# A depthwise convolution's shifted copies: sixteen on-chip transfers per block, or five by way of DRAM

## The reference

```python
glu = z[..., :o1] + b_glu
u = glu[..., :D_CONV] * jax.nn.sigmoid(glu[..., D_CONV:])
...
uc = jnp.concatenate([u_past, u], axis=1)
y = lax.conv_general_dilated(uc, w_dw[:, None, :], window_strides=(1,), padding='VALID',
                             dimension_numbers=('NWC', 'WIO', 'NWC'),
                             feature_group_count=D_CONV) + b_dw
y = jax.nn.silu(layer_norm(y, ln_g, ln_b))
return y @ w_pw + b_pw, uc[:, -(CONV_WIDTH - 1):]
```

## Time and profile before

| | us |
|---|---|
| median of 3 runs | 2307.46 |
| all runs | 2057.3, 2307.46, 2405.7 |
| the profiled execution's own time | 2060.45 |
| its span (slowest core, core 0) | 2058.9 |
| the other even cores (2, 4, 6) | 2051.0, 2048.2, 2048.6 |
| the odd cores (1, 3, 5, 7) | 1991.4, 1991.4, 1993.9, 1990.5 |
| PE busy on core 0 | 1924.8 (93%) |
| DVE, ACT, POOL busy on core 0 | 799.2, 366.5, 152.1 |

### The profile page before, as it was taken

One profiled execution on the slowest core, in us unless ns is written; L12 is line 12 of the kernel. 1 busy time (PEld: TensorE's weight loads), 2 busy tenths in 40 slices (PEclk: granted clock), 3 DMA queues, 4 the chain that ended last, 5 costly groups with the idle time before them and its releaser, 6 DMA issues.

```text
span 2058.9 us, 33059 instructions; the slowest of 8 cores (1990.5 to 2058.9 us)
## 1 busy us (share of the span) xinstructions
PE 1924.8 (93%) x12474; PEld 1119.9 (54%) x12474; DVE 799.2 (39%) x1349; ACT 366.5 (18%) x679; POOL 152.1 (7%) x176
## 2 busy tenths in 40 slices
PE   4789899987878999999999999999999999999997
PEld 2344454654544566666446565655656556565653
DVE  2546656644424622223243414234142341423126
ACT  2422121321222522222043000000000000000013
POOL 0000100110111010000000000000000000000000
PEclk9999999999989999999999999999999999999999
DMA  7853766996776386467867997877967556544404
GB/s 199 168 90 73 139 136 144 219 195 133 121 122 90 45 134 98 77 119 117 236 82 148 165 184 123 168 128 135 184 112 121 78 78 83 79 72 61 77 5 165
DMA packets 218970, 252.28 MB, mean 123 GB/s; under 512 B 8944, under 2 KB 190896, under 8 KB 214788
## 3 DMA queue, kind: packets, MB, share of 16 engines
q0 software_dynamic: 193216, 137.77, 49.3%
q1 hardware_dynamic: 22973, 66.01, 9.8%
q10 hardware_dynamic: 2616, 46.28, 7.8%
HBM read 365.16 MB, written 58.67 MB: 206 GB/s over the span
## 4 chain that ended last, share of the span: by engine, by line
PE 86%; DMA 5%; DVE 3%; issue 2%; ACT 2%; SPq 1%; ACTq 1%; DVEq 0%; POOL 0%; POOLq 0%
PE ps L202 86%; SPq L223 1%; DMA aW<-w_in 1%; DMA aU<-aubb 1%; DMA aq<-aqlow 1%; DMA ardb<-dnd 1%; DVE auP L202 1%; ACTq L223 0%; DMA atab<-tab 0%; DVE ahb L202 0%; ACT ahb L202 0%; DMA dnd<-aden 0%; DVE axacc L202 0%; ACT L202 0%; ACT ajunk L202 0%
## 5 line engine op out<-in xcount | busy, mean ns | idle before, releaser
L202 PE MATMUL ps<-amixT,aHW 128*128 128x352 bf16 x4224 | 632.0, 313 | 0.0
L202 PEld LDWEIGHTS ps<-amixT,aHW 128*128 128x128 bf16 x4224 | 412.9, 98 | 218.2 <-issue 0.2
L202 PE MATMUL ps<-ahT,aW 128*128 128x352 bf16 x2304 | 372.1, 321 | 1.8 <-DVE aubb L202 1.0
L202 PE MATMUL ps<-aHW,aaq 128*128 128x512 bf16 (+1 forms) x1584 | 318.2, 380 | 1.4 <-DVE aaq L202 0.4
L202 PEld LDWEIGHTS ps<-ahT,aW 128*128 128x128 bf16 x2304 | 228.2, 100 | 128.2 <-issue 3.8
L202 PE MATMUL ps<-aW,ahT 128*128 128x512 bf16 (+1 forms) x1296 | 283.4, 390 | 7.9 <-DMA aW<-w_in 4.8
L202 DVE TENSOR_TENSOR aaq<-ps,asgb 128x352 bf16<-128x352 f32 x132 | 69.3, 525 | 553.8 <-PE ps L202 553.8
L202 DVE TENSOR_TENSOR axacc<-ps,axacc 128x512 f32<-128x512 f32 x320 | 220.2, 691 | 66.1 <-PE ps L202 34.7
L202 PEld LDWEIGHTS ps<-aHW,aaq 128*128 128x128 bf16 (+1 forms) x1584 | 140.8, 98 | 176.4 <-issue 11.4
L202 PEld LDWEIGHTS ps<-aW,ahT 128*128 128x128 bf16 (+1 forms) x1296 | 133.9, 112 | 135.9 <-issue 25.5
L202 ACT ACTIVATE asgb<-ps 128x352 f32<-128x352 f32 x132 | 61.2, 464 | 819.8 <-PE ps L202 819.7
(11 more groups left out here) (156 smaller groups left out, 1088.9 us busy)
## 6 DMA issues: line engine op xcount, KB each, us to landing
aW<-w_in POOLq DMA_DIRECT2D x40, 1024.0 KB, 13.2
aHW<-w_gate POOLq DMA_DIRECT2D x22, 1024.0 KB, 11.0
aHW<-w_up POOLq DMA_DIRECT2D x22, 1024.0 KB, 17.4
aHW<-w_down POOLq DMA_DIRECT2D x22, 1024.0 KB, 13.6
aKr<-ck SPq DMA_DIRECT2D x36, 512.0 KB, 6.3
aVb<-cv POOLq DMA_DIRECT2D x36, 256.0 KB, 5.8
axb<-xown SPq DMA_DIRECT2D x8, 1024.0 KB, 8.7
axacc<-xown SPq DMA_DIRECT2D x8, 1024.0 KB, 14.4
```

The source lines that it names most:

```text
L202: self.q[eng].append(lambda e: getattr(e, meth)(*a, **kw).then_inc(s, 1))
```

## The change

`conv_in` no longer makes 16 copies on chip. One transfer writes the whole of `ubb[i_]` (128 rows of 1056 bf16 values) to a DRAM tensor `ubd[i_]`, and four transfers read it back, one for each shift `i`, each filling 32 partitions of `U4[i_]` for all four channel groups. The four wait for the write through the key `('ub', i_)`. All five are issued on SP's queue, in both roles and all blocks. In role a `conv_hist` is gone as a function; its steps stand in `rows_out`: first the row transpose, then the two history transposes, then ACT's copy of the history, of the rows, and of the new columns into `uc`. In `later` there is one function per block in place of two.

```diff
     def conv_in(n):
         i_ = n % 2
         S.op('dve', lambda e: e.tensor_tensor(out=dgc[i_], in0=mkap(idr, [[0, 32], [1, 32]]), in1=mkap(wtap[:, n, 0:1], [[1, 32], [0, 32]]), op=ALU.mult))
-        for g in range(4):
-            for i in range(4):
-                S.dma('act' if n >= 6 and not H and i % 2 else 'sp', U4[i_][32 * i:32 * i + 32, g, :], ubb[i_][32 * g:32 * g + 32, 8 * i:8 * i + 1032])
+        S.dma('sp', io['ubd'][i_], ubb[i_], writes=[('ub', i_)])
+        for i in range(4):
+            S.dma('sp', U4[i_][32 * i:32 * i + 32, :, :], bass.AP(io['ubd'][i_].tensor, 8 * i, [[1056, 32], [32 * 1056, 4], [1, 1032]]), reads=[('ub', i_)])
...
     def rows_out(n):
         rb_ = rowb[n % 2][0:NR, :]
         S.op('pe', lambda e: e.transpose(out=PS[6][0:NR, 0:128], in_=u2[n % 2][:, TGG[2][1] - NR:TGG[2][1]], identity=identf))
+        if not H:
+            c_ = uc[n % 2]
+            for a in range(2):
+                S.op('pe', lambda e: e.transpose(out=PS[6][:, 128 + 120 * a:248 + 120 * a], in_=straw[0:120, a, 128 * n:128 * n + 128], identity=identf[0:120, 0:120]))
+            S.op('act', lambda e: e.copy(out=c_[:, :, 0:30], in_=PS[6][:, 128:368].rearrange("p (s r) -> p s r", r=30)))
         S.op('act', lambda e: e.copy(out=rb_, in_=PS[6][0:NR, 0:128]))
         if H:
             S.dma('sp', io['convp'][:, 128 * n:128 * n + 128], rb_)
         else:
+            S.op('act', lambda e: e.copy(out=c_[:, :, 30:34], in_=u2[n % 2][:, 320:352].rearrange("p (s j) -> p s j", j=4)))
             S.dma('sp', bass.AP(io['convs'].tensor, 26 * 1024 + 128 * n, [[30 * 1024, 8], [1024, 4], [1, 128]]), rb_)
-
-    def conv_hist(n):
-        c_ = uc[n % 2]
-        for a in range(2):
-            S.op('pe', lambda e: e.transpose(out=PS[6][:, 128 + 120 * a:248 + 120 * a], in_=straw[0:120, a, 128 * n:128 * n + 128], identity=identf[0:120, 0:120]))
-        S.op('act', lambda e: e.copy(out=c_[:, :, 0:30], in_=PS[6][:, 128:368].rearrange("p (s r) -> p s r", r=30)))
-        S.op('act', lambda e: e.copy(out=c_[:, :, 30:34], in_=u2[n % 2][:, 320:352].rearrange("p (s j) -> p s j", j=4)))
...
                     conv_in(n)
-                    if not H:
-                        later.append(lambda: conv_hist(n))
                     later.append(lambda: rows_out(n))
...
+    io['ubd'] = [nc.dram_tensor("ubd%d" % i, [128, 1056], BF16).ap() for i in range(2)]
```

## The result

| | before | after |
|---|---|---|
| median of all runs, us | 2182.38 | 2030.11 |
| runs compared, us | 2054.83, 2057.3 | 2025.27, 2025.30, 2034.91 |
| the profiled execution, us | 2060.45 | 2034.91 |
| ratio, 95% interval | | 0.9863 [0.9818, 0.9908] |

The kernel became 1.4% faster, 28 us, and the interval keeps clear of 1 by twice its own half width. (In some executions one die's cores are held at a lower clock; these carry the median of before up to 2182 and are left out of every ratio, and of the medians given for the experiments.)

What follows compares the result with a forecast made beforehand. Role a's cores set the end, with 44.5 us of PE idle and lower clock from 455 to 680 us to win. Core 0: 5.0 + 4.0 + 7.9 - 0.3 + 8.1 + 4.5 = 29.2 off 2060.45, forecast 2031, range 2022 to 2046.

Steps and rivals of the forecast that it cites:

- the 8.98 at block 3's `aubb`: DVE's 8.98 us wait in block 1 for the copies before writing aubb for block 3; forecast to be gone.
- Everything hides: Rival, chance 0.18: Kr load in time, trip 7.1 us; block 1 gives 9.3, block 7 6.6; 2019.5 us.
- The round trip starves beside the weight loads: Rival, chance 0.12: at block 1 SP's ring moves 46 GB/s, Kr lands 15 us later; 2051 us.
- the bound of resolution: Claim that a measurement can tell about 2%, 41 us, from no change; chances 0.16 faster, 0.80 between, 0.04 slower.
- block 3, transposes: Row transpose no longer waits for ACT's copies into uc: 3.5 us of wait plus 1.5 of clock, 5.0 gained.
- block 4, conv: Convolution's 5.43 us wait for aU goes, plus 2.7 for faster matmuls: 8.1 gained on core 0.
- block 6, ACT's issues: PE's 6.38 us idle behind ACT's copy issues and copy into uc goes, plus 1.5 of clock: 7.9.
- block 7: 8.35 us gained, less a new 5.9 wait for the reads and 2.7 of slower matmuls: -0.3, bounds -5.4 to +6.6.
- block 1: Of 9.3 us on offer, 3.5 kept plus 1.0 of clock, as the stall moves to a late Kr load: 4.5.
- other small waits (the rest of the stage): Five further PE waits for auc, 5.5 us in all, less 1.5 left for a late u2: 4.0 gained.
- 5.1 and some 4: Block 1's write: 5.1 us for itself, some 4 for reads and a Kr load ahead; lands at about 481.
- the 0.3 for SP's wake-up: Allowance of 0.3 us in the DRAM trip, between the write's landing and the reads; quiet trip 11.3 us.

Runs made afterwards that it cites:

- after_again: The changed kernel run once more with no further change, on the same chip as later experiments: 2026.78 us, ratio 0.9871.
- fill_later: The changed kernel with the four reads of blocks 0 to 3 in role a issued one piece of columns later on SP's queue: 2019.55 us, ratio 0.9836.
- rows_only: The kernel before with only the new order of row and history transposes, the sixteen on-chip copies kept: 2041.87 us, ratio 0.9937.
- all_on_sp: The kernel before with all sixteen copies of every block issued on SP's queue, none on ACT's: 2047.65 us, ratio 0.9969.

## Why the prediction was right or wrong

**The time was right, and most of the mechanism, but part of that was luck.** 2031 was forecast; the runs lie at 2025.3 to 2034.9. These signs came: no wait for `auc`, no issues on ACT, the 8.98 at block 3's `aubb` replaced (7.34, and for the write), a wait before conv(7) of 6.69 where 5.9 stood, a product late through a Kr load near 490 (494.93). Others did not, or came from the list of what would be wrong: SP's waits for the write are 6.2 us on average and up to 10.7, not 3 to 5; the write took over 8 us up to the issue of its reads at three of core 0's eight blocks (8.1, 11.3 and 8.6 at blocks 0, 1 and 3); and conv(5) waited on core 6. The luck is that two terms missed in opposite directions, as the table below shows, and that the slowest run's 2034.91 was set by core 6, for which nothing had been forecast.

"Everything hides" fell at both of its places, block 1 and block 7. "The round trip starves beside the weight loads" fell by the view of the DMA queues on core 0 (packets, MB, share of 16 engines). Block 1's weight load goes out at 471.68 before and at 463.08 after, so what answers the earlier trace rows is the stretch from 462.4 to 483.4:

```profile
q1 hardware_dynamic: 953, 1.96, 35.2%
```

1.96 MB in 21 us is 93 GB/s, where before it was 100, beside the same 2.2 MB on the queue of the weight loads: SP's queue neither starved nor gained. The forecast's 100 GB/s about held, and the rival's 46 did not come.

**The step that failed is the bound of resolution**, "about 2% is what a measurement of this kernel can tell from no change", and with it the 0.80 on a time that can't be told from no change. What the runs showed in its place is a gain of 1.4% with an interval that keeps clear of 1. The intervals here are ±0.45% for the change and ±0.14 to 0.29% for the experiments, 3 to 9 us. Nothing in the material supported 41 us: the lowest run of before and the profiled execution, 2057.3 and 2060.45, were 0.15% apart, and the spread up to 2405.7 says nothing of how finely two kernels can be told apart. The forecast's own range, gains of 14 to 38 us, lay wholly outside such an interval. By the same cases and their chances, 0.70 of the forecast and 0.18 of "everything hides" belonged to a clear gain: near 0.9 for faster, not 0.16.

**The terms.** On core 0, from the stretches between casts and convolutions in the two timelines, before less after:

| term | predicted | measured |
|---|---|---|
| block 3, transposes | 5.0 | 5.9 |
| block 4, conv | 8.1 | 7.9 (wait 5.43, matmuls 2.5) |
| block 6, ACT's issues | 7.9 | 7.3 |
| block 7 | -0.3 | -1.2 |
| block 1 | 4.5 (0 to 9.3) | -1.4 |
| other small waits (the rest of the stage) | 4.0 | 8.1 |
| sum | 29.2 | 26.6 |

Four terms were sized within 1 us. Two were not, and these are the terms of the sum that failed: block 1 gave 5.9 less than charged and the small waits 4.1 more, so that the sum came out within 2.6 by luck.

*Block 1.* Its mechanism was named, but not its price or its scatter: from block 1's cast to block 2's, cores 0, 2, 4 and 6 gained -1.4, 7.4, 2.5 and -0.1 us in the profile after, and 4.8, 4.4, 2.8 and 2.4 in `after_again`. So 4.5 lies in the upper part of what came. The sum let the write land 9.3 us after the cast's end and the Kr load 25; both held in `after_again` (9.4 and 25.4 on core 0), while the profile after shows 16.0 and 31.7. The write's 16.0 are 4.6 until SP issued it and 11.3 to land. "5.1 and some 4" charged the queue for the bytes ahead of the write and left out that SP, held by block 0's write until 464.12 and then issuing what stood ahead, couldn't issue it. `fill_later` shows that the price was where the reads stood, not the trip as such.

*The small waits.* 4.0 charged the waits alone. Block 0, for instance, gained 2.3 to 2.6 on every even core, with a wait for `auc` of 0.6 only; the 16 matmuls behind it had taken 3.9 to 4.2 before and take 2.55. Here the clock came back behind short gaps too. The longer gaps that core 0 has ahead of block 0 aren't needed for it: on core 6 these gaps are alike (2.79 us before, 3.08 after) and PEclk is 1.00 up to the transposes in both, but behind them it is 0.81 before (461 to 470 us) and 1.00 after (464.4 to 470).

*Block 7's trip* took 12.6 from the cast's end where 11.3 was assumed; the write 5.3 up to the issue of the reads, against the 3 taken for quiet queues, and the reads 7.1 against 8.0. The queues were not quiet: weight loads ran beside the write, in the kernel before too (q0 held 75.8% of the engines from 637.1 to 642.4 us). So the 5.1 taken for writes beside weight loads was the one to use. At block 2 nothing else moved, and there the same write needed 2.6 us up to the issue of the reads, 2.2 to 2.6 on the four even cores. Core 0, from 603.4 to 608.7, and then from 507.7 to 510.4:

```profile
q0 software_dynamic: 1308, 0.66, 92.8%
```

```profile
q1 hardware_dynamic: 144, 0.27, 25.4%
```

No row of before shows the 0.3 for SP's wake-up; on core 6 the reads go out 0.07 to 0.13 us after the write's link in the chain ends. The Trainium skill's fit (page "DMA: Bandwidth & Descriptors", section "Anatomy of one DMA — SWDGE (gpsimd) path") is stated for transfers that GpSimd issues; used for these, which SP issues, it gave an estimated 2.6 for the write and 7.3 for the whole trip. Block 2's write agrees with it; block 7's trip, beside other traffic, took 12.3 from the write's issue, and there the measurement decides.

*Overlap.* The sum took block 6's wait as one gain with two causes removed, which is right for the whole change; `rows_only` and `all_on_sp` show that one would have been enough.

*Core 2*, forecast to gain 22.0, gained 28.2 in the stage, 7.4 of it at block 1. *Core 6* wasn't forecast at all and became the last: its gain in the stage was 16.7, with a trip of 24 us at block 5, beyond the 16.4 taken as the upper bound. The prediction had called block 5 the least sure, because its cast stands beside a weight load.

## What to carry to other kernels

When a queue's owner waits for a transfer, count what stands behind the wait: in this kernel the trip through DRAM cost little where PE had work to cover it, but the reads ahead of the next write and of the next load that PE's work hangs on cost 7 us, and moving the reads of four blocks one piece later gave them back. Two causes of one wait are one gain; try each alone before adding them up. Price a transfer by what runs beside it at its own place, not by an average over the stretch. And judge what a measurement can resolve from runs that agree, not from the spread of all that are shown.

## What was not expected of the hardware

Landing times on core 0, after, 425 to 700 us (count, KB each, median us from issue to landing; for waits total, times, longest):

```profile
aU<-ubd SPq DMA_DIRECT2D x32, 258.0 KB, 9.2
...
aKr<-ck SPq DMA_DIRECT2D x5, 512.0 KB, 12.1
...
ubd<-aubb SPq DMA_DIRECT2D x8, 264.0 KB, 6.0
```

The Kr loads in `fill_later`, the same core and stretch:

```profile
aKr<-ck SPq DMA_DIRECT2D x6, 512.0 KB, 8.9
```

SP's waits, after:

```profile
SPq L122 <- DMA ubd<-aubb: 49.3, 8, 10.7
```

The write of 264 KB takes about as long, in the median, as the 256 KB write of the earlier trace rows (6.0 against 5.1), but 11 us in block 1, behind reads; SP stood 49 us in eight waits for it. The Kr loads, 512 KB, land after a median of 12.1 us, and after 8.9 when those of block 1 go ahead of the reads. And the same program shows 166.6 to 178.4 us for one stage on four cores with the same work; with the reads moved, 161.1 to 162.7, and with conv(7) later too, 155.0 to 155.1. In this kernel, scatter between cores went with transfers that were only just late.
